# A conditioning product spread over the four column groups of TensorE's array

## The reference

```
s_c, s_cc = silu(c), silu(c_ctx)                       # 1024 numbers each
for l in range(2):
    sh1, sc1, g1, sh2, sc2, g2       = split(s_c  @ w_ada[l] + b_ada[l], 6)   # w_ada[l] is 1024 x 6144, fp32
    sh1c, sc1c, g1c, sh2c, sc2c, g2c = split(s_cc @ w_ada[l] + b_ada[l], 6)
    h = rmsnorm(x, norm_attn_g[l]) * (1 + sc1) + sh1    # and hc from xc with the c vectors
    y, yc = parallel_mixers(h, hc, ...)                 # two groups of attention heads, one output product
    x = x + g1 * y
    h = rmsnorm(x, norm_ffn_g[l]) * (1 + sc2) + sh2
    x = x + g2 * peer_ffn(h, p)                         # 128 experts picked per token out of 16384
    # and the same for xc with yc, except in the last layer
return rmsnorm(x, final_norm_g)
```

## Time and profile before

| | us |
|---|---|
| median of three runs | 3027.63 |
| lowest, highest | 3021.54, 3055.24 |
| span of the profiled execution | 3018.9 |
| PE busy | 2228.5 (74%) |
| DVE busy | 1859.8 (62%) |
| ACT busy | 1074.2 (36%) |
| POOL busy | 936.1 (31%) |
| of PE: passes of the conditioning product (L667), 384 | 184.9 |
| DMA | 976 MB, mean 323 GB/s |

### The profile page before, as it was taken

How to read it: one execution, slowest core, us unless ns; L and a number is a source line. 1 busy time by engine, 2 the same in 40 slices (tenths; PEclk the granted TensorE clock), 3 DMA queues, 4 the chain that set the end, 5 groups by cost and what they waited for, 6 DMA issues and landing times.

```text
span 3018.9 us, 25891 instructions
## 1 busy us (share of the span) xinstructions
PE 2228.5 (74%) x6672; PEld 1108.8 (37%) x6672; DVE 1859.8 (62%) x4486; ACT 1074.2 (36%) x2975; POOL 936.1 (31%) x868
## 2 busy tenths in 40 slices
PE   6996578658878879667768877777765787666765
PEld 2534323433434435333323323233443343332322
DVE  0134776685458758886775555453577585767765
ACT  2022344434245534333342233232234353333332
POOL 0001233223234333233443434330023333344553
PEclk8997789889989899889889989888877888788887
DMA  5455699788887699799999999994278989889997
GB/s 186 129 175 195 271 370 349 304 333 329 293 328 287 264 377 355 310 409 380 386 401 415 381 400 406 392 400 151 63 290 335 357 317 363 337 346 418 406 413 316
DMA packets 203288, 976.17 MB, mean 323 GB/s; under 512 B 18300, under 2 KB 30104, under 8 KB 104856
## 3 DMA queue, kind: packets, MB, share of 16 engines
q0 software_dynamic: 110592, 805.36, 66.4%
q1 hardware_dynamic: 92568, 169.32, 16.3%
HBM read 973.56 MB, written 1.05 MB: 323 GB/s over the span
## 4 chain that ended last, share of the span: by engine, by line
PE 40%; DMA 31%; DVE 16%; issue 6%; ACT 4%; POOL 2%; SPq 1%; POOLq 0%; DVEq 0%; PEldq 0%; ACTq 0%; PEld 0%
DMA EXPERT<-in_peer_uv,FIX 20%; PE VS L847 14%; PE PA L713 9%; DMA WT<-in_peer_wq 7%; PE PB L835 5%; DVE EXPERT L1423 4%; PE PB L667 4%; DMA WT<-in_w_ada 2%; DVE SCR L1075 2%; PE PA L741 2%; POOL EXPERT L594 1%; DVE ACC L1433 1%; PE PA L789 1%; DMA WT<-in_w_in 1%; PE PB L781 1%
## 5 line engine op out<-in xcount | busy, mean ns | idle before, releaser
L847 PE MATMUL VS<-EXPERT,DIAG 128*128 128x512 f32 x2304 | 1148.8, 650 | 264.0 <-ACT DIAG L1030 253.0
L1423 DVE CUSTOM_DVE_ANT_0 EXPERT<-EXPERT,H 128x1024 f32<-128x1024 f32 x768 | 925.9, 1224 | 509.8 <-DMA EXPERT<-in_peer_uv,FIX 502.0
L594 POOL DMA_INDIRECT EXPERT<-in_peer_uv,FIX x768 | 891.9, 1161 | 1016.0 <-PE VS L847 538.5
L847 PEld LDWEIGHTS VS<-EXPERT,DIAG 128*128 128x128 f32 x2304 | 464.1, 210 | 900.9 <-issue 540.0
L1023 ACT ACTIVATE GEL<-DOT 128x1 f32<-128x1 f32 x768 | 154.5, 201 | 1023.6 <-DVE DOT L1423 1015.6
L713 PE MATMUL PA<-WT,HT 128*128 128x512 f32 (+2 forms) x768 | 329.7, 585 | 53.4 <-ACT QTD L960 19.8
L586 POOL COPY FIX<-IDX 128x8 uint32 (+1 forms) x96 | 44.0, 458 | 1035.6 <-PE VS L847 590.0
L835 PE MATMUL PB<-HT,WT 128*128 128x128 f32 (+1 forms) x1280 | 207.0, 329 | 157.7 <-DMA WT<-in_peer_wq 157.7
L1030 ACT ACTIVATE DIAG<-IDN,WEI 128x128 f32<-128x128 f32 x576 | 231.3, 402 | 130.1 <-PE VS L847 113.6
L835 PEld LDWEIGHTS PB<-HT,WT 128*128 128x128 f32 x1280 | 193.7, 222 | 167.6 <-issue 160.3
L1433 DVE SCALAR_TENSOR_TENSOR ACC<-EXPERT,WEI,ACC 128x1024 f32<-128x1024 f32 x192 | 246.0, 1281 | 2.2 <-ACT WEI L1025 1.8
(11 more groups left out here) (137 smaller groups left out, 1641.3 us busy)
## 6 DMA issues: line engine op xcount, KB each, us to landing
WT<-in_w_ada SPq DMA_DIRECT2D x96, 512.0 KB
WT<-in_peer_wq SPq DMA_DIRECT2D x80, 512.0 KB
WT<-in_w_in SPq DMA_DIRECT2D x56, 512.0 KB
WT<-in_w_out SPq DMA_DIRECT2D x40, 512.0 KB
EXPERT<-in_peer_uv,FIX POOLq DMA_INDIRECT x768
WT<-in_w_in SPq DMA_DIRECT2D x16, 384.0 KB
WT<-in_w_in SPq DMA_DIRECT2D x20, 288.0 KB
WT<-in_mla_wk_up SPq DMA_DIRECT2D x5, 512.0 KB
```

Of the source, the lines that this page charges most:

```text
L594: pool.indirect_dma_start(out=EXPERT[:, j, :], out_offset=None, in_=a["peer_uv"], in_offset=bass.IndirectOffsetOnAxis(ap=FIX[:, par, j:j + ...
L847: ins = nc.tensor.matmul(VSUM[n][:, :], DIAG[:, i, :], EXPERT[:, j, D + n * W:D + (n + 1) * W], start=first, stop=last_one)
L1423: nc.vector.tensor_tensor_reduce(out=EXPERT[:, j, 0:D], in0=EXPERT[:, j, 0:D], in1=H2[:, b % HB, :], scale=1.0, scalar=0.0, op0=ALU.mult, ...
```

## The change

`ST` becomes 128 x 8 x 32: for each k the two silu columns and 30 columns of zeros. Product k writes to partitions 32 (k mod 4) to 32 (k mod 4) + 31 of the bank, that is, it uses column group k mod 4 of the array; k = 0 to 3 start the four sums and k = 4 to 7 end them. So the bank holds four partial sums of each row. ScalarE copies all 128 partitions. In `adat`, the four transposes are replaced by four products of MROW (128 x 128, stationary) with `SEL` (128 x 2), which has a 1 where a partition's number mod 32 is 0 (first column) or 1 (second): it turns and adds the four partial sums at once. `SEL` is made by one reduction over the identity matrix, and ST is set to zero first. Last, the cost of a run in the table that deals out the experts' stages goes from 50 to 20.

```diff
--- before.py
+++ after.py
@@ -34,6 +34,7 @@
 NB = 3
 WSLOTS = 4
 KP = 2
+QUAD = 32
 RING = 8
 HB = 3
 UNIT = 8
@@ -161,7 +162,7 @@
 
 COST = {"stat": (45, 0), "norm": (50, 0), "in": (0, 40), "turn": (0, 10), "root": (5, 5), "up": (0, 25), "attn": (35, 0),
         "hnorm": (20, 0), "heads": (20, 0), "gates": (10, 0), "out": (0, 50), "back": (20, 0), "pick": (85, 0), "also": (80, 0),
-        "ada": (50, 0), "adat": (5, 0), "mod": (5, 0)}
+        "ada": (20, 0), "adat": (5, 0), "mod": (5, 0)}
 PER_TILE = {"in": 4, "turn": 4, "root": 4, "up": 4, "out": 4}
 
 
@@ -407,8 +408,9 @@
         GD = sb("GD", [P, 4, P])
         DIAG = sb("DIAG", [P, BY_PE, P])
         COL = sb("COL", [P, 2, 2 * MODS])
-        ST = sb("ST", [P, 2, KD])
-        MROW = sb("MROW", [2, 2, W])
+        ST = sb("ST", [P, KD, QUAD])
+        SEL = sb("SEL", [P, 2])
+        MROW = sb("MROW", [P, 2, W])
         MOD = sb("MOD", [P, DEPTH, MODS, 2])
         SKT = sb("SKT", [P, DEPTH * 2, P])
         LS = sb("LS", [P, 2 * DEPTH])
@@ -664,7 +666,8 @@
                 for k in range(KD):
                     if k % KP == 0:
                         w = piece()
-                    last = nc.tensor.matmul(bank[0:2, :], ST[:, :, k], w[:, k % KP, :], start=(k == 0), stop=(k == KD - 1))
+                    rows = slice(k % 4 * QUAD, k % 4 * QUAD + QUAD)
+                    last = nc.tensor.matmul(bank[rows, :], ST[:, k, :], w[:, k % KP, :], start=(k < 4), stop=(k >= KD - 4))
                     if k == 0:
                         release()
                     if k % KP == KP - 1 and k < KD - 1:
@@ -678,7 +681,8 @@
                 pe.wait_ge(mrow_ready, tick("mrow"))
                 bank = fill_a()
                 for k in range(4):
-                    last = nc.tensor.transpose(bank[:, 2 * k:2 * k + 2], MROW[:, n % 2, k * P:(k + 1) * P], IDN[0:2, 0:2])
+                    last = nc.tensor.matmul(bank[:, 2 * k:2 * k + 2], MROW[:, n % 2, k * P:(k + 1) * P], SEL[:, :],
+                                            start=True, stop=True)
                 last.then_inc(filled_a, 1)
 
             def norm(stage):
@@ -895,14 +899,14 @@
                 bank = from_b()
                 nc.scalar.copy(SKT[:, :, :].rearrange("p i n -> p (i n)"), bank[:, :]).then_inc(emptied_b, 1)
                 act.wait_ge(cols_set, 1)
-                nc.scalar.activation(ST[:, :, :].rearrange("p c k -> p (c k)"), COL[:, 0, 0:2 * KD], ACT.Silu)\
+                nc.scalar.activation(ST[:, :, 0:2], COL[:, 0, 0:2 * KD].rearrange("p (c k) -> p k c", c=2), ACT.Silu)\
                     .then_inc(silu_done, 1)
                 act.wait_ge(lam_sums, 2 * DEPTH)
                 nc.scalar.activation(LE[:, :], LS[:, :], ACT.Exp).then_inc(lam_exps, 1)
 
             def ada(stage):
                 bank = from_b()
-                nc.scalar.copy(MROW[:, stage[2] % 2, :], bank[0:2, :]).then_inc(emptied_b, 1)
+                nc.scalar.copy(MROW[:, stage[2] % 2, :], bank[:, :]).then_inc(emptied_b, 1)
                 act.wait_ge(emptied_b, rb.n)
                 act.sem_inc(mrow_ready, 1)
 
@@ -1077,7 +1081,9 @@
             def consts(_):
                 nc.vector.memset(EPST[:, :], EPS)
                 nc.vector.memset(ONES[:, :], 1.0)
+                nc.vector.memset(ST[:, :, :], 0.0)
                 dve.wait_ge(consts_in, CONSTS_ALL)
+                nc.vector.tensor_reduce(SEL[:, :], IDN[:, :].rearrange("p (j r) -> p r j", j=4)[:, 0:2, :], AX_X, ALU.add)
                 bank = from_a()
                 nc.vector.tensor_copy(COL[:, 0, 0:ROWS], bank[:, 0:ROWS]).then_inc(cols_set, 1)
                 dve.wait_ge(cols_set, 1)
```

## The result

The changed kernel takes 3063.93 us (median of four runs, 3056.97 to 3077.83) where the kernel before takes 3031.57 with the run that was added on the same chip: a ratio of 1.0115, 95% interval 1.0061 to 1.0169. It is slower, by about 35 us by the ratio (the medians lie 32 apart); I had forecast 2992, and a range that ends at 3025. The span of its profiled execution is 3060.1 us against 3018.9.

What follows compares the result with a forecast made beforehand. The changed product is 6% of the span; transfers hide nine of its 24 runs, and late weight pieces bound others. Attention 15, head 8.5, 400 to 500 7, 1200 to 1400 3: 33.5 off 3018.9 gives 2985.4, 2992 between scales; range 2962 to 3025.

Steps and rivals of the forecast that it cites:

- Overlap of column groups: In one run, fp32 passes in separate column groups overlap entirely: 1.9 us instead of 7.03; no-overlap rival 3034, chance 0.12.
- No drain: Rival denied here: each change of column group drains TensorE, passes 0.59 us apart instead of 0.43; 3063 us, chance 0.05.
- The fourth piece as bound: Between attention steps a run waits for its fourth weight piece: 3.9 us; rival without this bound 2975, chance 0.10.
- The head: Kernel start, 14 to 52 us, four runs: X issued earlier, then transfers bound; saves 8.5 us, bounds 6 and 11.
- Attention: First context attention, 158 to 226 us, six runs: saves 20.0, less 3 for transposes, 2 for waits and clock; net 15.
- 400 to 500: Window in us with two runs among the expert rows' products: 12 us less TensorE, 7 taken, range 0 to 12.
- 1200 to 1400: Window in us with three runs, the one of 1235.21 in the chain of waits: saves 3, bounds 0 and 8.
- Nothing from the nine runs in the saturated stage: Nine runs, 1400 to 2014 us, DMA busy 0.99: their 69.7 us of TensorE gain nothing, as transfers hide them.
- The table of costs: A run counts 20, not 50, so experts' products are dealt earlier or later: 0 us, bounds plus and minus 8.
- the large move: At head 4, near 1250 us: block 1's close and block 2's first products go behind the pick; taken as 0.
- the order hurts: Rival: VectorE has nothing to multiply for two picks at head 4, small moves lose too; 20 us, 3012, chance 0.08.

Runs made afterwards that it cites:

- e1_cost50: The change with a run's cost back at 50, so every stage stands where it stood before, column groups kept: 3002.63 us, ratio 0.9916 to the kernel before.
- runs 4 and 6: Not follow-ups: the first and third of six runs of the changed product in the first context attention; 3.5 and 3.9 us forecast, 3.8 measured in e1_cost50.
- run 5: Not a follow-up: the second of six runs of the changed product in the first context attention; 4.4 us forecast, 6.6 measured in e1_cost50.
- run 7: Not a follow-up: the fourth of six runs of the changed product in the first context attention; 3.9 us forecast, 4.7 measured in e1_cost50.
- e3_early_slot: e1_cost50 plus the slot of a run's last piece given back behind the next attention step's first product: 2997.0 us, ratio 0.9896 to the kernel before.
- Runs 8 and 9: Not follow-ups: the last two of six runs of the changed product in the first context attention; 3.9 us each forecast, 3.9 and 4.4 measured in e1_cost50.
- run 3: Not a follow-up: the last of four runs of the changed product at the kernel's head; end forecast at 43.3 us, measured at 46.4 in the change.
- e11_layer0_groups: e1_cost50 with all eight products of each layer 1 run in one column group: 3001.32 us, ratio 0.9925 to the kernel before.
- e2_order_only: The kernel before with only a run's cost changed from 50 to 20, products as before: 3081.4 us, ratio 1.0164.
- e12_head4_close: e1_cost50 with block 1's last six expert products moved ahead of a run, its close and four experts' stages behind both picks of head 4: 3017.06 us.
- e8_one_quad: e1_cost50 with the one experts' stage ahead of the pick of head 6 of the latent tiles put behind it: 3014.98 us, ratio 0.9963 to the kernel before.
- e6_weave3: e1_cost50 with cost 20 only in the third of three calls dealing out experts' stages (blocks 2 and 3 over layer 1): 3016.35 us, ratio 0.9964.
- run 14: Not a follow-up: a layer 1 run of the changed product, ahead of the pick of head 6; in e8_one_quad its pieces are used from 1359.53 to 1376.24 us.

## Why the prediction was wrong

The range missed, and the sign. Point by point, by its steps; what e1_cost50 shows is the change's products without the order.

*Overlap of column groups: right.* Sixteen passes in 1.92 us, where I took 1.9, and the 0.70 us pair of the earlier trace rows had pointed to it. The Trainium skill's figure for three column tiles (TensorE: Matmul & The Clock Gate, section Measured speedup vs the span model) gave an estimate of 2.3 to 3; 7.03 over 1.92 is 3.66 times for four, nearer to full overlap.

*No drain: right.* The next attention product starts at 158.39, 0.07 us ahead of the modelled end of the last pass, the same distance as before the change. The Trainium skill's drain at a change of mode (TensorEngine Tiling, section Key Properties) doesn't show as a gap here. That this rival's time, 3063, is what was measured is chance: its mechanism isn't in the trace.

*The fourth piece as bound: right for the first runs.* In e1_cost50 runs 4 and 6 take 3.8 us, I had said 3.5 and 3.9; run 5, whose pieces come one after another, 6.6 (6.1 in the change) instead of 4.4; run 7 takes 4.7. e3_early_slot confirms the cause. Runs 8 and 9 take 3.9 and 4.4 us without a wait for weights in the list: there the granted clock is 0.64 and 0.69. So those two came near my 3.9 for another reason than mine. The six take 27.2 us together, where I had added up 23.5. The summing product costs 0.95 us against 0.41 before (1.70 at the lower clock); I had taken 0.9.

*The head: 5.5 us instead of 8.5.* X went out where I said, 20.38 against 20.4, and TensorE resumed at 32.79 against 33.0. What I had too fast are the last pieces: run 3 ended at 46.4, not 43.3, so the saving lies below my lower bound of 6 by half a microsecond. I had also misread the start: the first six passes of the kernel before are 0.7 to 0.86 us apart, not ten or so, and its first two pieces took 5.8 us and not 3.4.

*Attention: 12.5 us in e1_cost50, 5.6 in the profiled execution of the change, where I said 15 within 9 and 20.* Both have the same instructions in this stretch, so the order is not what parts them. Part of the difference is the clock, as I had feared for this term; what made it fall earlier in one execution is not known. The change's trace first, then e1_cost50's (granted clock third from the end):

```profile
175.00:185.00 10.00, 10.00 (x42) 7.01 (x42) 4.48 (x17) 1.77 (x6) 0.00 (x0) 0.55 0.44 151
```
```profile
175.00:185.00 10.00, 8.31 (x56) 4.71 (x54) 4.15 (x17) 2.93 (x10) 0.00 (x0) 1.00 0.71 248
```

With TensorE at 1.2 GHz for most of these 10 us, the change gets 42 passes done, e1_cost50 at 2.4 GHz gets 56.

*400 to 500: 7 said, about 6 measured* (e1_cost50 against the kernel before goes from 18 us ahead at addition 0 to 24 at addition 12). *1200 to 1400: 3 said, none measured.* *Nothing from the nine runs in the saturated stage: right, as closely as the runs tell.* e11_layer0_groups shows no loss without their groups, and in e1_cost50 the 614 us that answer to the earlier trace rows have DMA at 0.99 again with 30 us less of TensorE:

```profile
1375.00:1989.00 614.00, 441.58 (x1147) 193.89 (x1145) 371.80 (x735) 211.48 (x643) 235.14 (x225) 0.85 0.99 400
```

So the sum of these terms, 33.5 us, stands against 25 us (16 to 34 by the interval; the traces' 5.5, 12.5, 6 and 0 make 24): somewhat too large, head and attention above all.

*The table of costs: this step failed.* I wrote "I take 0, bounds plus and minus 8". It is worth 61 us between the change and e1_cost50, and 50 between e2_order_only and the kernel before. The wrong part is not the view of the large move: I had listed that VectorE would have two picks of work, that the ring would fill in about 26 us and that DMA idled there already. I then set the new idle time equal to the old one, by a sum of mean rates. The trace says one slice against two: TensorE and VectorE each have both picks ahead of the close and of the products that free the slots, and in e12_head4_close the close adds 13.8 us between the pick and the products, in which GpSimd waits a second time. It cost 14 us. The second error was the count: I looked at one large move and called the others small because they were one place long. The e8 move is one place long and costs 12 us; there a run that waits for its own weights stands just ahead. And third, I priced no move in the stage where DMA is busy 0.99, and in e6_weave3's expectation I read the prediction as saying that nothing can be lost there. What full transfers hide is TensorE's time. They don't hide a ring that stands full: the third dealing costs 14 us, some 6 of it in that very stage, where DMA's share falls.

The rival "the order hurts" named the mechanism, with 0.08 and at 20 us. It had DMA idle for 5 us more at head 4, where the move costs 14, and the small moves at a few times as much together. Both the price of a place and the number of places were too low.

*What stays open.* For the two moves of the second dealing the loss is followed, move by move, to what holds the slots. For the first and the third dealing (22 and 14 us) the traces show that the time is idle time of DMA, all of it in the first and some 6 us in the third, but not which moves make it; of the first, one move was tried alone and costs 4 us or nothing. Which of the others carry the rest wasn't tried.

## What to carry to other kernels

A cost that steers where other work is dealt is a change of order, and has to be priced as one: list each place at which something has moved, and for each ask what releases the ring that feeds the saturated resource, and what now stands ahead of it. A stage moved by a single place can cost half of what the faster product gains (12 us of 25 here), and the same kind of move can cost next to nothing elsewhere (4 us, not told from none). Keep the two edits apart: the faster product with the old cost gains 0.8%, with the "truer" cost it loses 1.1%; and after the edit look for the next bound of the thing made faster, here, between attention steps, the slot that was given back one stage too late.

## What the runs showed of the hardware

Four fp32 products of 128 x 32 by 128 x 512 in the four column groups run at once: 16 passes in 1.92 us instead of 7.03, and a pair in 1.05 us, although each streams its own 128-partition operand. I had only seen it for row halves, whose operands share the partitions among them.

Pieces of weights that stand against gathers arrive about 6 us apart. In e8_one_quad SyncE issues four pieces within 2.33 us from 1350.24, TensorE waits for each of the four of run 14, and uses them at 1359.53, 1365.51, 1371.52 and 1376.24; the last spacing is 4.7 us. e1_cost50 has 6.1, 6.1 and 3.8 us at the same place. 512 KB in 6 us is 87 GB/s of the 414 that flow from 1366 to 1372. In the first attention, without gathers, one piece took 3.4 us from its issue to its last bytes.
